# Expert weights in runs of 16 KB: two mixture-of-experts layers on one Trainium2 core

## The reference

```
hid = silu(xe @ w_gate) * (xe @ w_up)     # xe: the rows of tokens that this expert serves
ye  = hid @ w_down
```

## Time and profile before

| | |
|---|---|
| median of the runs | 2827.58 us |
| the profiled execution: its time, its span | 2823.28 us, 2821.5 us |
| PE busy | 2405.8 us, 85% |
| DVE, ACT busy | 1265.4 us, 978.7 us |
| mean rate of the DMA engines | 287 GB/s |
| DMA packets | 242410, of which 410 of 8 KB or more |
| stage 1 | from 1399 to 1861 us of the span |
| stage 2 | from 2335 to 2811 us of the span |

### The profile page before, as it was taken

How to read it: one execution, slowest core, us unless ns; L and a number is a source line. 1 busy time by engine, 2 the same in 40 slices (tenths; PEclk the granted TensorE clock), 3 DMA queues, 4 the chain that set the end, 5 groups by cost and what they waited for, 6 DMA issues and landing times.

```text
span 2821.5 us, 31643 instructions
## 1 busy us (share of the span) xinstructions
PE 2405.8 (85%) x12971; PEld 1503.4 (53%) x12971; DVE 1265.4 (45%) x2017; ACT 978.7 (35%) x1552; POOL 93.4 (3%) x155
## 2 busy tenths in 40 slices
PE   5977787589999999598899999979889968777687
PEld 3745655478888887453443434348577652222222
DVE  2478446489999998446300000035665450000001
ACT  3345323277778887324100000034354330000000
POOL 1010300100000000200000000000000000000000
PEclk8989988799999999799899999989999989999998
DMA  9279910289999997656599999953013568999997
GB/s 343 90 276 331 366 63 26 92 312 392 394 393 392 392 385 284 232 194 248 218 409 409 409 409 409 409 216 120 30 51 106 193 229 318 409 409 409 409 409 280
DMA packets 242410, 809.04 MB, mean 287 GB/s; under 512 B 10211, under 2 KB 10377, under 8 KB 242000
## 3 DMA queue, kind: packets, MB, share of 16 engines
q1 hardware_dynamic: 226688, 753.88, 69.4%
q0 software_dynamic: 12000, 37.15, 3.7%
q10 hardware_dynamic: 3568, 15.88, 1.4%
HBM read 775.27 MB, written 31.60 MB: 286 GB/s over the span
## 4 chain that ended last, share of the span: by engine, by line
PE 64%; DMA 19%; DVE 9%; ACT 3%; issue 3%; SPq 1%; DVEq 0%; POOL 0%; PEldq 0%; ACTq 0%; PEld 0%; POOLq 0%
PE PS L256 61%; DMA ring<-in_w_e_down 7%; DMA ring<-in_moe_w_up 4%; DMA ring<-in_w_e_up 3%; DMA ring<-in_w_e_gate 2%; PE PS L2223 1%; DVE hgrn L1024 1%; DMA ring<-in_moe_w_gate 1%; DMA ring<-in_moe_w_down 1%; SPq L395 1%; DMA ring<-in_ada_w 1%; DVE hgrn L1014 1%; PE PS L571 0%; DVE SM L2859 0%; DVE cut L431 0%
## 5 line engine op out<-in xcount | busy, mean ns | idle before, releaser
L431 DVE TENSOR_TENSOR cut<-ring,cut 128x1024 fp32r<-128x1024 f32 x492 | 584.1, 1220 | 251.1 <-ACT cut L423 239.8
L423 ACT CAST cut<-ring 128x1024 fp32r<-128x1024 f32 x492 | 508.9, 1053 | 344.5 <-PE PS L256 316.7
L256 PE MATMUL PS<-cut,xeT 128*128 128x512 f32 x1536 | 364.7, 394 | 3.2 <-DVE cut L431 3.2
L256 PEld LDWEIGHTS PS<-cut,xeT 128*128 128x128 f32 x1536 | 285.8, 189 | 67.7 <-DVE cut L431 6.3
L256 PE MATMUL PS<-ring,XE 128*32 128x512 f32 x1008 | 228.6, 608 | 63.2 <-DMA ring<-in_w_e_up 41.5
L256 PE MATMUL PS<-ring,hidT 128*64 128x512 f32 (+1 forms) x1024 | 231.7, 605 | 50.4 <-DMA ring<-in_w_e_down 40.6
L256 PE MATMUL PS<-ring,xeT 128*64 128x512 f32 x1024 | 230.8, 600 | 15.4 <-DMA ring<-in_moe_w_gate 8.3
L256 PE MATMUL PS<-cut,parts 128*128 128x512 f32 x864 | 212.1, 408 | 28.0 <-DVE cut L431 18.3
L256 PE MATMUL PS<-parts,cut 128*128 128x512 f32 x864 | 204.7, 397 | 3.6 <-DVE cut L431 3.6
L256 PEld LDWEIGHTS PS<-cut,parts 128*128 128x128 f32 x864 | 169.2, 197 | 72.1 <-issue 18.9
L4018 DVE TENSOR_TENSOR X<-X,PS 128x512 f32<-128x512 f32 x8 | 5.1, 684 | 421.3 <-PE PS L256 421.3
(11 more groups left out here) (568 smaller groups left out, 2605.6 us busy)
## 6 DMA issues: line engine op xcount, KB each, us to landing
ring<-in_moe_w_gate SPq DMA_DIRECT2D x64, 2048.0 KB, 12.3
ring<-in_moe_w_up SPq DMA_DIRECT2D x64, 2048.0 KB, 12.4
ring<-in_moe_w_down SPq DMA_DIRECT2D x64, 2048.0 KB, 12.2
ring<-in_w_e_up SPq DMA_DIRECT2D x32, 2048.0 KB, 23.5
ring<-in_w_e_down SPq DMA_DIRECT2D x32, 2048.0 KB, 23.6
ring<-in_w_e_gate SPq DMA_DIRECT2D x31, 2048.0 KB, 23.5
ring<-in_ada_w SPq DMA_DIRECT2D x24, 2048.0 KB, 12.1
ring<-in_w_in SPq DMA_DIRECT2D x13, 2048.0 KB, 7.8
```

What stands on the lines that cost most here:

```text
L256: return pe.matmul(o, l, r, start=start, stop=stop, **kw)
L423: act.copy(self.bufs[i % len(self.bufs)][0], w).then_inc(self.high.sem, 1)
L431: dve.tensor_tensor(low, w, high.bitcast(F32), ALU.subtract).then_inc(self.low.sem, 1)
```

## The change

All 192 pieces of the two stages take another order of rows. With `four_rows`, partition p of a piece reads the rows 4p to 4p + 3, which lie one behind the other: one run of 16 KB in place of four of 4 KB. Chunk c of a piece now holds the rows 4p + c. So that the products sum the same pairs, the activations are turned in the same order: where 128 neighbouring columns of the tokens or of `hid` were the stationary operand of a product or transpose, now every fourth of 512 is (`by_fours`: the 128 values are 16 bytes apart). Sizes, counts and order of all instructions, the slots and the waits stay.

```diff
+    def four_rows(w, h):
+        return w[512 * h:512 * h + 512, :].rearrange("(p c) n -> p c n", c=4)
+
+    def by_fours(a):
+        return a.rearrange("p (a n f) -> p a f n", n=P, f=4)
...
-            W.add((1, e, m, h), cols(moe[m][1, e], 0, k0=512 * h, k=4, width=D), "pe", k=4, width=D)
+            W.add((1, e, m, h), four_rows(moe[m][1, e], h), "pe", k=4, width=D)
...
-                        W.add((2, e, m, h), cols(last_experts[m][0, e], 0, k0=512 * h, k=4, width=D), "pe", k=4, width=D)
+                        W.add((2, e, m, h), four_rows(last_experts[m][0, e], h), "pe", k=4, width=D)
...
-                        last = mm(bank(0)[:, 64 * k:64 * k + 64], H[:, c, k * P:(k + 1) * P],
+                        last = mm(bank(0)[:, 64 * k:64 * k + 64], by_fours(H[:, c, :])[:, k // 4, k % 4, :],
                                   picks[m % 2][:, 64 * c:64 * c + 64], c == 0, c == 1)
...
-                    last = pe.transpose(bank(3)[:, j * P:(j + 1) * P], hid[i][:, j * P:(j + 1) * P], ident)
+                    last = pe.transpose(bank(3)[:, j * P:(j + 1) * P], by_fours(hid[i])[:, 0, j, :], ident)
...
-                ins = mm(bank(k), part(c)[:, k * P:(k + 1) * P], SS[:, c, :, :].rearrange("p e s -> p (e s)"),
+                ins = mm(bank(k), by_fours(part(c))[:, k // 4, k % 4, :], SS[:, c, :, :].rearrange("p e s -> p (e s)"),
                          first and c == 0, last_ and c == 1)
...
-                    last = pe.transpose(bank(6 + h)[:, k * P:(k + 1) * P], hid[i][:, h * 512 + k * P:h * 512 + (k + 1) * P], ident)
+                    last = pe.transpose(bank(6 + h)[:, k * P:(k + 1) * P], by_fours(hid[i])[:, h, k, :], ident)
```

More of the change, by code:

```diff
@@ L2017, in late_sync @@
                         sp.wait_ge(*late_used(6 * m - 6 + (k if k else NS)))
-                    v = moe[mt][layer].rearrange("e (c p) n -> p e c n", p=P)
+                    v = moe[mt][layer].rearrange("e (a p c) n -> p e a c n", a=2, c=4)
                     sp.dma_start(ring_t[:, k % NS * SLOT:(k % NS + 1) * SLOT].rearrange("p (e c n) -> p e c n", e=1, c=4),
-                                 v[:, bass.ds(expert, 1), 4 * h:4 * h + 4, :]).then_inc(late_in[k % NS].sem, 16)
+                                 v[:, bass.ds(expert, 1), h, :, :]).then_inc(late_in[k % NS].sem, 16)
             def late_tensor(m):
@@ L2025, in late_tensor @@
                 for j in range(8):
-                    last = pe.transpose(bank(3)[:, j * 64:(j + 1) * 64], late_xe[i][0:64, j * P:(j + 1) * P], ident[0:64, 0:64])
+                    last = pe.transpose(bank(3)[:, j * 64:(j + 1) * 64], by_fours(late_xe[i][0:64, :])[:, j // 4, j % 4, :], ident[0:64, 0:64])
                 last.then_inc(late_x_turned.sem, 1)
```

## The result

The changed kernel takes 2882.84 us (median of four runs, 2878.94 to 2887.89) against 2828.07 before: a ratio of 1.0199, 95% interval 1.0179 to 1.0220. The forecast was 2791, the range ended at 2834. The changed kernel is 55 us slower.

A forecast was written before the change was run, and what follows sets the result against it. Weight streams bound stage 2; PE and stream lie close in stage 1. Gains of 16.0 us (stage 1) and 20.5 (stage 2), 36.5 in all, strided loads at 0, gave 2827.6 - 36.5 = 2791 us; range 2782 to 2834.

The forecast's parts named there:

- The bounds of the kernel before: Weight stream limits stage 2; in stage 1, PE (27.8 us per expert) and stream (30.8 us) are close limits.
- The runs: Weight streams of both stages: 16 KB packets take 612 ns, 428 GB/s; stage 1 ends 16.0 us earlier, stage 2 20.5.
- Rival 2: Weight streams of both stages: longer runs bring no rate, 409 GB/s stays; 2827 us; chance 0.12.
- The strided loads: Stationary operands 16 bytes apart on PE's path in stage 1: bounded between zero and 102 ns more each, taken as 0.
- The two rows that it leaned on: DVE reading every second value, 8 bytes apart, in 404 to 429 ns; moved operands passing 2.3 values a ns.
- The rival that stood for the price: Rival 1: strided loads on PE's path in stage 1 cost as much again; 2853 us; chance 0.17.
- The rule of lines: SBUF is read in 16-byte lines; crossing to a new line pays a penalty unless a line is hit at least twice.
- Rival 1: PE's path in stage 1: strided loads cost 107 ns more each, 3.85 us per expert; 2853 us; chance 0.17.
- The choice: 32 products of 226 ns cover loads of 114 ns; doubled loads would be level, so 0 to 1 us.
- the sign: In the profile after, 32 loads of a pick at 7 us, not 3.65, would make Rival 1 true.

The follow-up runs named there:

- e2: The changed kernel with the weights in 16 KB runs but 128 neighbours as stationary operands, so wrong pairs are summed: 2787.06 us, ratio 0.9850.
- e4: The changed kernel with two neighbouring rows per run (8 KB) and every second value, 8 bytes apart, as stationary operand: 2800.46 us, ratio 0.9905.
- e1: The changed kernel with its strided stationary operands but the weights laid out as before, so wrong pairs are summed: 2901.51 us, ratio 1.0264.
- e3: The change made in stage 2 alone, stage 1 left as in the kernel before: 2804.38 us, ratio 0.9918.
- e5: The changed kernel's 16 KB runs, but ACT and DVE reorder while copying out of PSUM and PE loads neighbours: 2790.02 us, ratio 0.9868.
- e7: The changed kernel with the pick cut to half of its loads from the second expert on: 2826.16 us, one timed run.

## Why the prediction was wrong, point by point

**The bounds of the kernel before: right.** Stage 2 hung on the stream, stage 1 on two limits close together. With faster runs alone (e2) PE takes over stage 1, as forecast.

**The runs: right.** 612 ns a packet and 428 GB/s were forecast from runs of 2 KB, 4 KB and one store of 16 KB; measured 612 and 428. Stage 2's stream is 19.2 us shorter (20.5 forecast). By e2 stage 1 ends at 1844.3 (1845.0), so 16.6 us earlier (16.0); that it fits to 0.7 us is in part luck. The prediction took fifteen periods of 27.83 us, but the last one has no pick in it and took 25.1 in e2, 2.7 less; and the first down product of e2 began at 1422.44, 2.0 later than the 1420.44 that it started from. A slip in reading without effect: a packet of 4 KB took 164.4 ns by the earlier trace rows, not 164.0. e4 adds the point in between, 421 GB/s at 8 KB, on the same line. Rival 2 falls.

**The strided loads: the step that failed.** The prediction bounded the price at zero below and 102 ns above, for want of a row with a gap in a stationary operand, and said "I take 0". For the loads of the picks it is 122 ns (7.54 us less 3.65, over 32), above even the upper bound; e1, with these loads alone, is 74 us slower than before. The two rows that it leaned on didn't reach the case. Line 1024 reads with a gap of 8 bytes, and e4 shows that 8 bytes are nearly free for a load too; 16 are not. And the rate of the moved operand, 2.3 values a ns, is a rate of neighbours: it tells how fast values that lie together can be had, and nothing of values that lie apart. Such a row is no evidence at all for the gap in question. The rival that stood for the price was given 0.17. The rule of lines that the prediction quoted for it from the Trainium skill (SBUF — State Buffer, "Door 1: The DMA port swizzle") described the picks rightly.

**Rival 1 came true, and came short.** It placed the cost rightly, on PE's path in stage 1, at 3.85 us per expert for 36 loads of 107 ns. Measured are 3.99 us at full clock: 3.90 for the 32 of a pick, more than it had, and 0.09 for the four transposes, far less than its 0.43. In the changed kernel fifteen picks x 3.90, sixteen sets of transposes x 0.09 and 0.65 us for the first pick, which ran at half clock before as well, are 60.6 us: by the loads alone stage 1 would end at 1845.0 + 60.6 = 1905.6, where rival 1 had 1906.6. That the two agree to 1 us is luck, since its errors in the pick and the transposes cancel. The stage ends at 1937.5. The rest is what no part of the prediction had, the clock: 1.90 us in each of the fifteen down products that a pick precedes (the last one kept its 7.1 us), 0.32 in the four transposes ahead of it and 0.04 in the step behind them, 33.9 us in all. That is why the result lies at 2883 and not at 2853. The loads and the clock are 94.5 us of new work on PE's path. Added to the end of stage 1 in e2, 1844.3, less the 1.0 us by which the first pick began earlier here (1392.07 against 1393.07), they give 1937.8, and the trace has 1937.5.

**The choice: right for the loads, short for the clock.** 0 to 1 us were given for the 32 products. In e3 they took 9.15 us, 0.06 more than the 9.09 before. In the changed kernel the chain has 10.57 us for them, 1.48 more, over the upper bound; the granted clock there was 0.71 on average where it was 0.82 before and 0.84 in e3, which has the same loads. So this is the clock again; what held it down for longer there stays open. The whole way from stage 1 to stage 2 grew by 0.4 us only: 0.7 more ahead of the choice, 1.5 in it, and 1.7 less from its end to the first held issue (10.6 us, 12.3 before).

**What would show it.** The list named the sign, 7 us for the 32 loads of a pick, and so it is (7.54). The clock was not on the list.

## What to carry to other kernels

Price a new layout on both of its sides. Here the longer runs of the weights are worth 37 to 41 us (e5, e2; 428 GB/s in place of 409), and the strided reads that paid for them cost some 94 us of TensorE's path, a third of it by the clock that fell behind them, in a stage with only 3 us per expert between its two limits. Put a reordering where a copy out of PSUM happens anyway (e5, 37 us faster than before) and leave TensorE's loads with neighbours; of the two gaps measured here, 8 bytes was nearly free for 32-bit values (e4) and 16 bytes was not. And where no row shows an operation in the form that it will have, a row of another form is no ground for taking the cheap end.

## What the runs showed of the hardware that was not expected

- A product's load of 128 x 128 values with gaps of 16 bytes takes 236 ns at either clock: 16 of them took 3.81 us in e7, the first 2.99 of these at 1.00, and the first pick of the changed kernel runs at 0.50 all through and takes 7.54 us for 32. Loads of neighbours took 6.90 us there and 3.65 at full clock. So a load of neighbours goes with TensorE's clock and this one does not.

```profile
1391.60:1399.80 8.20, 7.73 (x32) 7.54 (x32) 6.97 (x40) 0.00 (x0) 0.00 (x0) 0.50 1.02 417
```
```profile
1392.07 7.54 PEld L256 LDWEIGHTS PS<-SM,H 128*128 128x128 f32 x32 [0.72 <-DVE SM L1839]
```

- A transpose's load with the same gap is another case: four strided transposes lost 0.09 us at full clock (0.58 us against 0.49), some 20 ns each.
- During slow loads the granted clock fell though PE shows as busy all the time (1.00 to 0.50 some 3 us after they begin), and the work behind them pays: 2.26 us per expert here.
- ACT and DVE read PSUM with gaps of 16 bytes as fast as neighbours (597 and 688 ns for 128 x 512, as before).
- Packets cost 84.7, 160.2, 311 and 612 ns for 2, 4, 8 and 16 KB (387, 409, 421 and 428 GB/s over 16 engines): near 75.5 ns for each 2 KB and 9 ns for each packet.
